# A mixture-of-experts layer whose first two pairs of experts get their tokens from a sort of their own

## What is computed

```python
g_prob = softmax(tok @ w_rg + b_rg)
g_w, g_idx = top_k(g_prob, 1)
e_sel = (tok @ w_re + b_re).reshape(N, 4, 8)[arange(N), g_idx[:, 0]]
e_w, e_idx = top_k(softmax(e_sel), 2)
expert = (g_idx * 8 + e_idx).reshape(-1)
order = argsort(expert)
xs = tok[order // 2]
hg = ragged_dot(xs, w_gate, sizes)
hu = ragged_dot(xs, w_up, sizes)
ys = ragged_dot(silu(hg) * hu, w_down, sizes)
```

## Time and profile before

| what | value |
|---|---|
| median of three runs | 1099.21 us (1095.69 to 1100.38) |
| the profiled execution | 1098.14 us, span 1096.4 us |
| mean granted TensorE clock | 0.993 of full |
| PE busy | 1064.1 us (97%) |
| DVE, ACT, POOL busy | 689.5, 521.6, 101.6 us |
| DMA | 253.76 MB, 231 GB/s in the mean, about 415 GB/s from 880 us on |

### The profile page before, as it was taken

The page is one execution under the profiler, slowest core; times in us unless marked ns, Lnnn a source line. Parts: engine busy times, 40 slices in busy tenths (PEclk is TensorE's granted clock), DMA queues, the critical chain, the costliest instruction groups (busy, mean ns, idle before and its releaser), DMA issues.

```text
span 1096.4 us, 20817 instructions
## 1 busy us (share of the span) xinstructions
PE 1064.1 (97%) x8482; PEld 919.6 (84%) x8482; DVE 689.5 (63%) x1305; ACT 521.6 (48%) x912; POOL 101.6 (9%) x169
## 2 busy tenths in 40 slices
PE   8999999999999999999999999999999999999995
PEld 6888899999999888889999999998999655555452
DVE  5685788888854767598889966787556611111114
ACT  4544666655644454486665555674553211121113
POOL 5010000000000000010000003000100031222210
PEclk9999999999999999999999999999998999999998
DMA  9664576777655545476776556644357699999994
GB/s 274 218 225 154 155 231 166 214 219 209 211 174 181 156 164 173 136 226 197 203 234 198 170 171 203 170 154 130 98 203 321 247 417 416 415 414 414 415 414 167
DMA packets 201919, 253.76 MB, mean 231 GB/s; under 512 B 21968, under 2 KB 181265, under 8 KB 189537
## 3 DMA queue, kind: packets, MB, share of 16 engines
q1 hardware_dynamic: 187406, 223.65, 60.1%
q0 software_dynamic: 14000, 28.63, 7.7%
q10 hardware_dynamic: 419, 0.16, 0.1%
HBM read 274.39 MB, written 11.55 MB: 261 GB/s over the span
## 4 chain that ended last, share of the span: by engine, by line
PE 80%; DVE 8%; DMA 5%; ACT 5%; issue 2%; SPq 0%; DVEq 0%; ACTq 0%; POOLq 0%
PE ps L920 18%; PE ps L921 17%; PE ps L922 17%; PE ps L3098 10%; PE ps L3111 5%; DMA we<-in_w_exp_gate 2%; DMA over_wlo<-in_w_exp_gate 2%; DVE wlo L874 1%; PE ps L813 1%; ACT whi L854 1%; PE ps L2652 1%; PE ps L3072 1%; ACT xhi L879 1%; PE ps L2913 1%; PE ps L3141 1%
## 5 line engine op out<-in xcount | busy, mean ns | idle before, releaser
L920 PE MATMUL ps<-xhi,whi 128*128 128x272 f32 (+2 forms) x1312 | 386.1, 294 | 7.5 <-DVE xlo L889 3.0
L921 PE MATMUL ps<-xlo,whi 128*128 128x272 f32 (+2 forms) x1312 | 375.2, 286 | 0.0
L922 PE MATMUL ps<-xhi,wlo 128*128 128x272 f32 (+2 forms) x1312 | 374.1, 285 | 0.0
L874 DVE TENSOR_TENSOR wlo<-raw,whi 128x2048 fp32r<-128x2048 f32 (+1 forms) x112 | 252.1, 2252 | 96.1 <-ACT whi L854 95.8
L854 ACT ACTIVATE whi<-raw 128x2048 fp32r<-128x2048 f32 (+1 forms) x112 | 210.8, 1883 | 174.9 <-PE ps L922 174.4
L920 PEld LDWEIGHTS ps<-xhi,whi 128*128 128x128 f32 x1312 | 247.2, 188 | 16.4 <-issue 12.4
L921 PEld LDWEIGHTS ps<-xlo,whi 128*128 128x128 f32 x1312 | 247.1, 188 | 1.1 <-issue 0.5
L922 PEld LDWEIGHTS ps<-xhi,wlo 128*128 128x128 f32 x1312 | 246.9, 188 | 0.0
L920 PE MATMUL ps<-hhi,whi 128*128 128x272 f32 (+2 forms) x384 | 110.5, 288 | 0.0
L921 PE MATMUL ps<-hlo,whi 128*128 128x272 f32 (+2 forms) x384 | 109.3, 285 | 0.0
L922 PE MATMUL ps<-hhi,wlo 128*128 128x272 f32 (+2 forms) x384 | 109.0, 284 | 0.0
(11 more groups left out here) (520 smaller groups left out, 1762.2 us busy)
## 6 DMA issues: line engine op xcount, KB each, us to landing
raw<-in_w_up SPq DMA_DIRECT2D x88, 512.0 KB, 5.2
raw<-in_w_in SPq DMA_DIRECT2D x32, 1024.0 KB, 5.4
ada<-in_w_ada POOLq DMA_DIRECT2D x48, 512.0 KB, 5.2
raw<-in_w_down SPq DMA_DIRECT2D x16, 896.0 KB, 4.5
raw<-in_w_exp_up SPq DMA_DIRECT2D x11, 1024.0 KB, 20.3
raw<-in_w_exp_gate SPq DMA_DIRECT2D x10, 1024.0 KB, 10.7
raw<-in_w_exp_down SPq DMA_DIRECT2D x10, 1024.0 KB, 14.9
raw<-in_w_out SPq DMA_DIRECT2D x8, 1024.0 KB, 5.0
```

What stands on the lines that cost most here:

```text
L874: dve.tensor_tensor(wlo[SLOT[n]][:, 0:nk, :], raw[n % RAW][:, 0:nk, :], whi[SLOT[n]][:, 0:nk, :].bitcast(F32), ALU.subtract).then_inc(s_w_ ...
L920: pe.matmul(dst, ah, bh, start=first, stop=False, **kw)
L921: pe.matmul(dst, ah, bl, start=False, stop=False, **kw)
L922: return pe.matmul(dst, al, bh, start=False, stop=last, **kw)
```

## The change

- The first two pairs (256 slots) get a sort of their own, in fixed windows: slot = 64 x expert + rank in that expert, for the tokens of experts 0 to 3. `first_place` has 256 columns, and PE makes the same 32 products with it (`FIRST = 256`), into eight banks. ACT and DVE write the result straight into `xsl` (4 evictions each), without `Xs` and without the window copies. Pair 0's gates wait for it tile by tile.
- The ranks no longer wait for the offsets: `ranked` is formed first, and the offsets come after it, by way of ACT (which now copies `nbS` and `offn`).
- The full sort of 512 columns remains. Its tiles 0 and 1 are sorted after pair 0's ups, 2 and 3 after pair 1's ups, 4 to 7 after pair 1's downs; the full `place` is made on DVE behind the first evictions. Pair 2's gates are the first that read `Xs`.
- The inverse map moves from behind pair 0's ups to behind tile 7; with it `row_of(0)` and `overflow()` move on DVE from p = 0 to p = 2, ahead of pair 1's `y_right` and pair 2's `hu`.
- The turn of pair 1 stands alone, ahead of pair 1's downs, and pair 2's gates follow the inverse map.
- `hu` is written packed (`hu[:, j, :]`, read strided from PSUM) and `hut` is in two other places.
- Three of the four `low_part` steps move ahead of DVE's wait for the logits, and POOL's fill of `Yb` with zeros moves from behind the inverse map to behind the logits.
- The order of the weight loads and their buffers are as before.

```diff
-SORT_BANK = [0, 1, 2, 4, 5, 7, 3, 6]
-EARLY = 6
+FIRST_BANK = [0, 1, 2, 3, 5, 7, 4, 6]
+SORT_BANK = [3, 6, 0, 3, 1, 4, 0, 3]
+FIRST = 4 * 64
...
+            pool.wait_ge(s_routed.sem, s_routed.after())
+            fill(Yb[:, 1, :], 0.0)
...
             pool.wait_ge(s_dest.sem, s_dest.after(0))
-            fill(Yb[:, 1, :], 0.0)
...
+            act.wait_ge(s_moe_sums.sem, s_moe_sums.after("counted"))
+            act.activation(nbS[:, :], ps[6][0:NEXP, 0:P], ACT.Copy).then_inc(s_count_copied.sem, s_count_copied.event())
+            act.wait_ge(s_moe_sums.sem, s_moe_sums.after("offsets"))
+            act.activation(offn[:, :, :].rearrange("p k e -> p (k e)"), ps[6][:, P:P + 2 * NEXP], ACT.Copy).then_inc(s_offn.sem, s_offn.event())
             for k in range(0, KT, 2):
+                act.wait_ge(s_sorted.sem, s_sorted.after("first", k))
+                act.activation(xsl[:, :, :, k, :], ps[FIRST_BANK[k]][:, 0:FIRST].rearrange("p (a h n) -> p a h n", a=2, h=2),
+                               ACT.Identity, bias=rt[:, 1, 128 + k:129 + k], scale=rt[:, 0, 128 + k:129 + k]).then_inc(s_slot_a.sem, s_slot_a.event("first", k))
...
+                if p == 2:
+                    slots_even(4)
+                    slots_even(6)
+                    take_a(2)
+                    take_a(3)
...
-                if p + 2 < NPAIR:
+                if p < 2:
+                    slots_even(2 * p)
+                elif p + 2 < NPAIR:
                     take_a(p + 2)
...
             r(dve.memset(rt[:, :, 0:8], -3.0e38))
+            low_part(0, 0)
+            low_part(1, 0)
+            low_part(0, 1)
             dve.wait_ge(s_routed.sem, s_routed.after())
...
+            for t in range(2):
+                r(dve.tensor_scalar(first_place[:, t, :], iota[:, 1:FIRST + 1], R(t, 66, 67), None, ALU.is_equal))
+                dve.scalar_tensor_tensor(first_place[:, t, :], iota[:, 1:FIRST + 1], R(t, 67, 68), first_place[:, t, :].bitcast(F32), ALU.is_equal, ALU.add).then_inc(s_place.sem, s_place.event("first", t))
+            for k in range(1, KT, 2):
+                dve.wait_ge(s_sorted.sem, s_sorted.after("first", k))
+                dve.tensor_scalar(xsl[:, :, :, k, :], ps[FIRST_BANK[k]][:, 0:FIRST].rearrange("p (a h n) -> p a h n", a=2, h=2),
+                                  rt[:, 0, 128 + k:129 + k], rt[:, 1, 128 + k:129 + k], ALU.mult, ALU.add).then_inc(s_slot_b.sem, s_slot_b.event("first", k))
...
             for p in range(NPAIR + 1):
                 f, q, kind = phase_at(p)
+                if p == 2:
+                    slots_odd(5)
+                    slots_odd(7)
+                    take_b(2)
+                    take_b(3)
+                    dve.wait_ge(s_moe_sums.sem, s_moe_sums.after("inverted"))
...
+                    overflow()
                 if p >= 1:
                     y_right(PAIRS[p - 1])
...
-                    dve.tensor_tensor(hu[:, :], ps[p % 2][:, 256:512], sg[:, :], ALU.mult).then_inc(s_hu.sem, s_hu.event(p))
+                    by_turn = lambda w: w.rearrange("p (n j) -> p j n", j=2)
+                    dve.tensor_tensor(hu, by_turn(ps[p % 2][:, 256:512]), by_turn(sg[:, :]), ALU.mult).then_inc(s_hu.sem, s_hu.event(p))
...
+            unread(4, 7)
             for t in range(2):
...
+                pe.wait_ge(s_htk_lo.sem, s_htk_lo.after(1, t))
+                pe.wait_ge(s_place.sem, s_place.after("first", t))
+                for k in range(KT):
+                    if k == KT - 1 and t == 0:
+                        pe.wait_ge(s_offn.sem, s_offn.after())
+                    for u, src in enumerate((htk_hi, htk_lo)):
+                        o = pe.matmul(ps[FIRST_BANK[k]][:, 0:FIRST], src[:, t, k::KT], first_place[:, t, :], start=(u + t == 0), stop=(u + t == 2))
+                    if t:
+                        o.then_inc(s_sorted.sem, s_sorted.event("first", k))
...
-                if p == 1:
-                    turn(0)
-                elif p < NPAIR:
-                    widen("ga", p, turns)
+                if p == 0:
+                    widen("ga", p)
+                elif p in (1, 2, NPAIR):
+                    turn(p - 1)
                 else:
-                    turn(p - 1)
+                    widen("ga", p, turns)
                 if p >= 1:
                     narrow(p - 1)
-                if p == 1:
+                if p == 2:
+                    for k in range(4, KT):
+                        sort(k)
+                    invert()
+                if p in (1, 2):
                     widen("ga", p)
                 if p < NPAIR:
                     widen("gb", p)
+                if p < 2:
+                    sort(2 * p)
+                    sort(2 * p + 1)
```

More of the change, by code:

```diff
@@ L304, in build @@
         early_end = top[0]
+        wr_at = top[0]
         wr = sb("wr", [P, KT, 36])
@@ L2561, in _ @@
                     y_right(OVERS[q])
[L2562 to L2566, removed]
                 if p == 1:
@@ L3060, in _ @@
[L3060 to L3066, removed]
@@ new lines, in sort @@
+            def sort(k):
+                if k == 0:
+                    pe.wait_ge(s_place.sem, s_place.after(1))
+                if k == 5:
+                    pe.wait_ge(s_y_left.sem, s_y_left.after(0))
+                if k in (3, 6):
+                    pe.wait_ge(s_xs_even.sem, s_xs_even.after({3: 0, 6: 2}[k]))
+                if k == 7:
+                    pe.wait_ge(s_xs_odd.sem, s_xs_odd.after(3))
+                for t in range(2):
+                    for u, src in enumerate((htk_hi, htk_lo)):
+                        o = pe.matmul(ps[SORT_BANK[k]][:, :], src[:, t, k::KT], place[:, t, :], start=(u + t == 0), stop=(u + t == 2))
+                o.then_inc(s_sorted.sem, s_sorted.event(k))
@@ new lines, in invert @@
+            def invert():
+                pe.wait_ge(s_at_rank.sem, s_at_rank.after())
+                pe.wait_ge(s_y_right.sem, s_y_right.after(0))
+                for s_ in range(4):
+                    for t in range(2):
+                        for j in range(2):
+                            for half_ in range(2):
+                                o = pe.matmul(ps[5][CAP * half_:CAP * half_ + CAP, NEXP * s_:NEXP * s_ + NEXP],
+                                              at_rank[:, t, j, CAP * s_:CAP * s_ + CAP], OHv[:, t, j, :],
+                                              start=(t == 0 and j == 0), stop=(t == 1 and j == 1))
+                o.then_inc(s_moe_sums.sem, s_moe_sums.event("inverted"))
@@ L3095, in halves_wide @@
+            def halves_wide(kind, bank, x, weights, ab, between=None, first=False):
                 cs = slice(0, 256) if kind == "ga" else slice(256, 512)
                 for j in range(8):
+                    if first and j % 2 == 0:
+                        pe.wait_ge(s_slot_a.sem, s_slot_a.after("first", j))
+                    elif first:
+                        pe.wait_ge(s_slot_b.sem, s_slot_b.after("first", j))
                     for half_, e in enumerate(ab):
```

160 lines of the change are left out of this document (65 added, 95 removed).

## The result

The changed kernel took **1107.38 us** (median of four runs, 1105.65 to 1108.64) beside 1097.72 us for the kernel before on the same chip. The ratio, estimated over all these runs, is 1.0078, 95% interval 1.0054 to 1.0102; the two medians by themselves lie 9.7 us or 0.88% apart. In a second set of six runs it took 1106.62 beside 1098.88: 1.0075 (1.0052 to 1.0098). So it is slower by 0.75 to 0.78%, where 1104.9 and +0.52% had been forecast.

What follows compares the result with a forecast made beforehand. Expert weight loads bound the tail once pair 2's downs free load 29's place. Load 29 landing at 906.9 against 901.46 (+5.4), plus or minus traffic taken as 0.3, gave +5.7 on 1099.21: 1104.9 us, range 1100.0 to 1108.5.

Steps and rivals of the forecast that it cites:

- The order of the three releases: Loads 15, 27, 29 wait for first gates, pair 2's ups, pair 2's downs; the downs set the end, +5.4 us.
- The first sort: Its 32 products of 256 columns, bound by strided weight loads, keep 0.244 us each: 7.9 us, to 851.1.
- rival 1: First sort bound by its columns: step 0.117 us, 4.2 us less, total 1100.7, no change; chance 0.17.
- Start, pairs 0 and 1: First sort starts at 843.2 against 845.00, 1.8 us gained; load 15 goes out at 854.7, 3.9 us earlier.
- The low parts ahead of the router and POOL's fill: Before the first sort: low-part steps in DVE's wait cost nothing; POOL's fill costs 0 to 0.8 us, taken as 0.
- Pair 2's ups end at 890.6: After the full sort's pieces and the inverse map, pair 2's ups end at 890.6 against 886.22.
- The stall: At pair 2's turn PE waits 2.8 us for the gate-up product, queued on DVE behind the overflow bookkeeping.
- Rival 3, the fallen clock: Clock falls in the 2.8 us wait at pair 2's turn; 5.7 us to downs double: +11.4, 1110.6; chance 0.07.
- The spare of 1.8 us: In the kernel before, load 29 would still land in time if issued up to 1.8 us after pair 2's downs.
- other traffic: A return and some overflow loads fall behind load 29 instead of ahead: 2.6 us in all, 0.3 taken.

Runs made afterwards that it cites:

- before, packed: Kernel before, old order, with token parts written packed and its 512-column sort reading packed tiles: 1098.59 us, ratio 0.9996 to the kernel before.
- packed, queues freed: Changed kernel with packed tiles in both sorts, pair 2's product and ACT's overflow copy moved, value loads early: 1100.29 us, ratio 1.0013 to the kernel before.
- first sort packed: Changed kernel, its first sort reading 128 elements side by side instead of every eighth: 1103.48 us, ratio 1.0048 to the kernel before.
- queues freed: Changed kernel with pair 2's product inside DVE's bookkeeping and ACT's overflow-token copy behind its copy of pair 2's turn: 1104.17 us, ratio 1.0047 to the kernel before.
- after, second profile: The changed kernel run again, file unchanged, in the second set of runs: 1106.62 us, ratio 1.0075 to the kernel before.
- product early: Changed kernel with pair 1's right half and pair 2's product moved into the middle of DVE's overflow bookkeeping: 1105.97 us, ratio 1.0063 to the kernel before.
- value loads early: Changed kernel with only the value loads of pairs 2 and 3 on ACT and DVE moved ahead of the last evictions: 1106.56 us, ratio 1.0078 to kernel before.
- unread in the stall: Changed kernel with 18 unread 128-column products on TensorE in the wait at pair 2's turn: 1107.84 us, ratio 1.0084 to the kernel before.
- load 15 held back: Changed kernel with weight load 15 made to wait until the full sort's first tile is done: 1108.35 us, ratio 1.0081 to the kernel before.
- the two kernels with the downs moved: Against "packed, queues freed": pair 2's turn and downs ahead of pair 3's gates (1102.85 us), or earlier inside them with gate products behind the downs (1104.78 us).
- the last run: Against "packed, queues freed": pair 2's turn and downs earlier inside pair 3's gates, gate products behind the downs: 1104.78 us, ratio 1.0055 to the kernel before.

## Why the prediction was right, and where its sizes were off

**The order of the three releases: right.** Set the end of pair 2's downs beside the landing of the last expert load (last DMA row of the chain of waits, start and length). This is the row of the kernel before:

```profile
1042.79 22.34 DMA over_wlo<-in_w_exp_gate
```

And that of the second profile of after:

```profile
1048.55 22.29 DMA over_wlo<-in_w_exp_gate
```

| kernel | downs of pair 2 end | last load lands | between |
|---|---|---|---|
| before, packed | 893.55 | 1063.91 | 170.36 |
| before | 894.93 | 1065.13 | 170.20 |
| packed, queues freed | 898.15 | 1068.12 | 169.97 |
| first sort packed | 899.81 | 1068.90 | 169.09 |
| queues freed | 900.81 | 1071.03 | 170.22 |
| after, second profile | 901.82 | 1070.84 | 169.02 |
| product early | 901.87 | 1071.25 | 169.38 |
| value loads early | 902.49 | 1071.90 | 169.41 |
| unread in the stall | 902.79 | 1073.59 | 170.80 |
| load 15 held back | 903.30 | 1072.76 | 169.46 |
| after, first profile | 906.20 | 1075.73 | 169.53 |

Twelve and a half microseconds of difference on the left, 1.8 in the last column (1.3 without the unread products, whose last load row took 24.12 us instead of some 22.3). Where the downs of pair 2 end sets the time, whatever moved them: the sort, the stall, the slot chain or the clock. Only the two kernels with the downs moved leave this line (173.3 and 175.2 us), because the next release then decides.

**The first sort: right.** 7.72 us against 7.9, and the weight load shown as the cause. The Trainium skill's page "Advanced Engine Details and Errata" (section "SBUF Cachelines") asks for at least two hits on each 16-byte line; elements 32 bytes apart give one, and the 338 ns against 191 agree with it. The page "TensorE: Matmul & The Clock Gate" (section "LDWEIGHTS (loading the stationary operand)") lets the load's time go by the number of columns alone; for two tiles of the same shape these runs measure 338 and 191, so there the measurement decides. The section "Back-to-back issue gap" of that page of the Trainium skill, which the prediction used for rival 1, gives its step for a product by itself; for a stream of loads and products it says that both set the spacing. These runs agree: 0.24 us with the 338 ns load, 0.12 with the 191 ns one.

**Start, pairs 0 and 1: right within 0.4 us.** Sort from 843.03 (843.2 forecast) to 850.75 (851.1); load 15 at 854.37 (854.7). The low parts ahead of the router and POOL's fill cost nothing, as put.

**"Pair 2's ups end at 890.6": 1.2 us short.** The step that failed is "DVE's last eviction (0.8) and the slot copies end at the same time" as the inverse map. Between them stand two value loads per engine, which I had not counted; in the kernel before, those ahead of its first slot copies stood in the router. Loaded early, they let load 27 go out 0.7 us sooner (40.38 us behind the first sort instead of 41.05), and the downs end 1.0 sooner. A second term was too small as well: the 32 products of the full sort took 2.26 + 2.27 + 4.25 = 8.78 us, where I had 7.8. A first sort that ended 0.35 earlier and two turns shorter by 0.2 each hid most of that.

**The stall: right.** 2.8 forecast, 2.76 measured, 2.8 by removal. What I had not seen is that it is held by two queues, DVE's product and ACT's copy, so that freeing the first gave only 1.7 us at the downs, and the second the other 1.1.

**Rival 3, the fallen clock: it occurred in the first profile**, at 2.9 us (half gates 3.61 for 1.88, downs 4.40 for 3.43, turn 0.69 for 0.44), not 5.7, and did not in four other profiles with the same stall (load 15 held back, again, packed first sort, and value loads early, where the stall was 2.4 us). How many of the other executions had it, is not known. Of the changed kernel's ten runs the five with a mean clock of 0.987 to 0.990 took 1107.65 to 1108.64 us, the five with 0.992 or 0.993 took 1104.80 to 1107.12; but the mean clock of the kernel before scatters too (0.988 to 0.995 in the second set). So what part of the difference between the medians is the clock's, these runs do not say.

**The spare of 1.8 us: mis-sized, as it seems.** The prediction took it from load 15, which landed 4.7 us after its issue. Load 29, issued into the dry queue, took longer in the changed kernel (its row in the first profile: size, us to landing):

```profile
raw<-in_w_exp_down SPq DMA_DIRECT2D x1, 1024.0 KB, 5.6
```

With 5.6 the spare is 901.46 - 5.6 - 894.93 = 0.9; over all runs with a dry queue the landing took 4.8 to 5.9, so 0.6 to 1.7. The last column agrees loosely: before's 170.20 less the changed kernel's 169.0 to 169.5 is 0.7 to 1.2, but "queues freed", whose queue ran dry too, stands at 170.22. I had 1.8 and charged 0.3 for other traffic, net 1.5 against about 0.9.

The sum mended by the runs: 5.7 + 1.0 to 1.2 (ups and downs of pair 2 later) + 0.6 (spare) = 7.3 to 7.5, an estimate. Between the medians it is 7.7 in the second set and 9.7 in the first (8.2 and 8.6 by the ratios). So the forecast was right in direction and mechanism, and a quarter or more too small.

## What to carry to other kernels

Here halving the moving columns halved the step only where the weight load was short (0.12 us with a load of 191 ns, 0.241 with 338): compare the load's row with the step before counting on it, above all when the stationary tile is read with a stride. When buffers come free in order, work out each release on its own; a gain ahead of a release that is not the last one is handed back in a dry queue. And before moving one operation out of a stall, follow every queue between it and the engine that waits: here the same late result stood in two.

## What the runs showed that was not expected

- A strided stationary tile of 128 x 128 f32 loads in 338 ns, a packed one in 191, at the same clock; the product rows stretch with it (404 against 282 ns for 256 columns).
- At 512 columns packed tiles gain almost nothing (0.244 to 0.234 us), and the engines that have to write the packed layout pay for it: DVE 1.14 instead of 0.75 us per half, ACT 2.11 instead of 1.09 per block.
- TensorE stood still for 2.4 to 2.8 us and kept its full clock in four profiles of five; in the fifth, and behind the 3.4 us of the last run, the clock fell to 0.50. In the router's stage the clock differed between executions of like kernels too (0.56 over 830 to 840 in one, 0.68 in the other, of the same file), and the first sort began 1.4 us apart (843.03 against 841.61). Two profiles are therefore best compared by stretches, not by absolute times.
- The value loads ahead of a slot copy show as rows of 0.2 to 0.55 us of the queue's time; moving four of them on two engines out of the way made 1.0 us of the chain.
